# Two attention stages in another order, and the rotary tables moved behind the first feed-forward stage

## The reference

```python
def sublayer(x, shift, scale, gate, g_pre, g_post, fn, res_weight):
    h = rmsnorm(x, g_pre) * (1 + scale[:, None, :]) + shift[:, None, :]
    return x + res_weight * gate[:, None, :] * rmsnorm(fn(h), g_post)

# GLA, 4 heads, key width 128, value width 256, chunks of 64 tokens
q, k, v, log_a = chunks(q) * DK ** -0.5, chunks(k), chunks(v), chunks(log_a)
b = jnp.cumsum(log_a, axis=3)
q_dec = q * jnp.exp(b)
k_dec = k * jnp.exp(-b)
att = jnp.where(causal, jnp.einsum('bhnid,bhnjd->bhnij', q_dec, k_dec), 0.0)
o_intra = jnp.einsum('bhnij,bhnjv->bhniv', att, v)
upd = jnp.einsum('bhncd,bhncv->bhndv', k * jnp.exp(b_last - b), v)
# state scan over chunks: state = dec * state + upd
o = o_intra + jnp.einsum('bhncd,bhndv->bhncv', q_dec, states)
...
o = rmsnorm(o, g_out).astype(h.dtype).reshape(B, S, vd)
return (o * jax.nn.silu(r)) @ w_out

# MLA, 8 heads, 128 plain + 64 rotary columns, two blocks of 128 queries
c_q = rmsnorm(h @ w_dq, g_q)
q_nope, q_rope = jnp.split((c_q @ w_uq).reshape(B, S, MLA_HEADS, 192), [128], axis=-1)
q_rope = apply_rope(q_rope, cos, sin)
s = einsum(qn, k_nope) + einsum(qr, k_rope)   # scaled, masked
p = softmax(s)
o = einsum(p, v)
return o @ w_out
```

## Time and profile before

| what | value |
|---|---|
| time of the runs | 2954.34 us median of 3 (2954.05 to 2954.44) |
| profiled execution | 2955.43 us, its span 2953.7 us |
| PE busy | 2591.3 us, 88% of the span |
| DVE busy | 1575.9 us, 53% |
| ACT, POOL busy | 627.2 us, 681.8 us |
| mean granted TensorE clock | 0.963 |
| DMA | 928.84 MB, 314 GB/s over the span |

### The profile page before, as it was taken

One profiled execution on the slowest core, in us unless ns is written; L12 is line 12 of the kernel. 1 busy time (PEld: TensorE's weight loads), 2 busy tenths in 40 slices (PEclk: granted clock), 3 DMA queues, 4 the chain that ended last, 5 costly groups with the idle time before them and its releaser, 6 DMA issues.

```text
span 2953.7 us, 25930 instructions
## 1 busy us (share of the span) xinstructions
PE 2591.3 (88%) x9487; PEld 1600.5 (54%) x9487; DVE 1575.9 (53%) x3431; ACT 627.2 (21%) x1822; POOL 681.8 (23%) x687
## 2 busy tenths in 40 slices
PE   6999979998999789999889877898978999777776
PEld 4874548855884558847555422563634646322222
DVE  3562234633451435642378895546597466984444
ACT  1000201001000110000023333343333343332222
POOL 1110000100010001100024454323354243444332
PEclk8999989999999879999999999999999999999999
DMA  9994516955793517964179999999999999999997
GB/s 336 321 362 158 196 57 231 354 209 192 261 358 135 174 57 274 327 234 148 59 310 420 421 421 420 419 401 421 420 421 400 420 418 421 421 400 422 421 421 317
DMA packets 248998, 928.84 MB, mean 314 GB/s; under 512 B 19709, under 2 KB 120341, under 8 KB 167974
## 3 DMA queue, kind: packets, MB, share of 16 engines
q0 software_dynamic: 100768, 669.09, 55.9%
q1 hardware_dynamic: 148102, 258.08, 24.5%
HBM read 926.07 MB, written 1.05 MB: 314 GB/s over the span
## 4 chain that ended last, share of the span: by engine, by line
PE 62%; DMA 21%; DVE 10%; ACT 3%; issue 2%; SPq 1%; POOL 1%; DVEq 0%; POOLq 0%
DMA ring<-in_peer_uv_dram,lamt 20%; PE psW L871 19%; PE psF L824 13%; PE psF L1145 11%; PE psW L805 4%; DVE ring L2208 4%; PE psW L1215 3%; PE psW L774 2%; PE psW L794 2%; DMA mring<-in_tail_w_dram 1%; POOL ring L618 1%; PE psW L1227 1%; ACT small L1510 1%; PE psM L700 1%; PE psW L1166 1%
## 5 line engine op out<-in xcount | busy, mean ns | idle before, releaser
L1145 PE MATMUL psF<-ring,p_diag 128*128 128x512 f32 x2048 | 961.9, 615 | 232.8 <-ACT p_diag L1514 232.6
L2208 DVE SCALAR_TENSOR_TENSOR ring<-ring,h 128x1024 f32<-128x1024 f32 x512 | 621.3, 1224 | 442.0 <-DMA ring<-in_peer_uv_dram,lamt 438.5
L618 POOL DMA_INDIRECT ring<-in_peer_uv_dram,lamt x512 | 579.5, 1132 | 1045.0 <-PE psF L1145 812.8
L1145 PEld LDWEIGHTS psF<-ring,p_diag 128*128 128x128 f32 x2048 | 381.1, 195 | 763.6 <-issue 391.5
L871 PE MATMUL psW<-hT,ring 128*128 128x256 f32 x2560 | 556.6, 379 | 0.0
L871 PEld LDWEIGHTS psW<-hT,ring 128*128 128x128 f32 x2560 | 486.1, 190 | 74.9 <-issue 10.0
L824 PE MATMUL psF<-ring,arena 128*128 128x512 f32 x768 | 335.0, 597 | 15.1 <-DVE arena L2137 11.9
L824 PEld LDWEIGHTS psF<-ring,arena 128*128 128x128 f32 x768 | 146.6, 191 | 200.8 <-issue 183.2
L1507 ACT ACTIVATE small<-small 128x2 f32<-128x2 f32 x256 | 52.0, 203 | 733.5 <-DVE ring L2208 733.4
L1514 ACT ACTIVATE p_diag<-ident,small 128x128 f32<-128x128 f32 x512 | 177.6, 394 | 8.4
L1400 ACT ACTIVATE arena<-psW 128x256 f32<-128x256 f32 x88 | 33.8, 384 | 603.5 <-PE psW L871 539.8
(11 more groups left out here) (297 smaller groups left out, 2116.2 us busy)
## 6 DMA issues: line engine op xcount, KB each, us to landing
ring<-in_ffn_w_gu_dram SPq DMA_DIRECT2D x88, 1024.0 KB, 8.1
mring<-in_tail_w_dram SPq DMA_DIRECT2D x56, 1024.0 KB, 9.1
mring<-in_mod_t_dram POOLq DMA_DIRECT2D x43, 1024.0 KB, 7.2
ring<-in_ffn_w_down_dram SPq DMA_DIRECT2D x20, 2048.0 KB, 9.5
mring<-in_ada_w_dram POOLq DMA_DIRECT2D x22, 1024.0 KB, 7.6
M<-in_mod_t_dram POOLq DMA_DIRECT2D x21, 1024.0 KB, 7.2
mring<-in_cond_w_dram POOLq DMA_DIRECT2D x17, 1024.0 KB, 8.7
ring<-in_gla_w_in_dram SPq DMA_DIRECT2D x6, 2048.0 KB, 8.9
```

Source lines behind the costliest of these rows:

```text
L618: pool.indirect_dma_start(out=pair(n % PAIRS), out_offset=None, in_=rows, in_offset=bass.IndirectOffsetOnAxis(ap=s_idx[:, c:c + 1], axis=0 ...
L1145: ins = pe.matmul(psF[:, b, f * HALF:(f + 1) * HALF], p_diag[:, n % PAIRS, :], row_v(n % PAIRS)[:, f * HALF:(f + 1) * HALF], start=(i == 0 ...
L2208: dve.scalar_tensor_tensor(row_u(c), row_u(c), 1.0, h[:, b, :], ALU.mult, ALU.mult, accum_out=p_dots[:, c:c + 1]).then_inc(dot_done, 1)
```

## The change

Four edits.

1. DVE's table code and ACT's two functions for it become `tables()`, and are called once the first stage's `ffn` has returned, that is behind its last `half_step` on DVE and its last Silu on ACT, and ahead of the stage's finish.
2. In gla the two k units are not copied. DVE multiplies each straight out of its PSUM bank, `g_eu` first, then `g_en`. `state_ready` 2 follows the second `g_eu` product, and a new count 3 the last `g_en` product; PE waits for 3 ahead of the scores. ACT takes the roots of half 0 when its two output units are stored, and those of half 1 later; DVE scales and gates each half by itself (`scaled_heads`); PE turns half 0, projects it, turns half 1, projects it (`project_block`).
3. In mla the rotary columns come before the plain ones, in the loads and on PE, and DVE's two rotations stand between the stores of the plain columns.
4. The attention loop of mla makes two scores ahead; in a step PE does turn(s), score(s + 2), value(s), and DVE masks s + 2 between the copy of the turned probabilities and the store of the value.

```diff
@@ stage_loads, mla
-            yield [(slot(i + 1, 3, D)[:, k, :].rearrange("p (h c) -> p h c", c=NOPE), w[:, k, :, 0:NOPE])
-                   for k in range(3)], st.u + 11
-            yield [(slot(i + 2, 3, 512)[:, k, :].rearrange("p (h c) -> p h c", c=ROPE), w[:, k, :, NOPE:])
+            yield [(slot(i + 1, 3, 512)[:, k, :].rearrange("p (h c) -> p h c", c=ROPE), w[:, k, :, NOPE:])
+                   for k in range(3)], st.u + 9
+            yield [(slot(i + 2, 3, D)[:, k, :].rearrange("p (h c) -> p h c", c=NOPE), w[:, k, :, 0:NOPE])
                    for k in range(3)], st.u + 13
@@ PE
+        def project_block(i, lhs, b):
+
+            for k in range(KD):
+                if b == 0 and k % 4 == 0:
+                    arrived(i + k // 4)
+                w = slot(i + k // 4, 4, D)
+                for f in range(2):
+                    ins = pe.matmul(psF[:, b, f * HALF:(f + 1) * HALF], lhs[:, k, b * P:(b + 1) * P],
+                                    w[:, k % 4, f * HALF:(f + 1) * HALF], start=(k == 0), stop=(k == KD - 1))
+                if b == 1 and k % 4 == 3:
+                    ins.then_inc(w_used, 1)
+                if b == 0 and k == KD - 1:
+                    ins.then_inc(first_ready, 1)
@@ PE gla, ahead of the scores
+            pe.wait_ge(state_ready, 3)
@@ PE gla, end
-            u = transposes(u)
-            have(u - 1)
-            project(st, i + 7, hT, KD)
+            for b in range(TB):
+                u = turn_block(u, b)
+                have(u - 1)
+                project_block(i + 7, hT, b)
@@ PE mla
-            u = by_weights(u, slot(i + 1, 3, D), m_cT, 3, 8)
+            u = by_tokens(u, slot(i + 1, 3, 512), m_cT, 3, 512)
             arrived(i + 2)
-            u = by_tokens(u, slot(i + 2, 3, 512), m_cT, 3, 512)
+            u = by_weights(u, slot(i + 2, 3, D), m_cT, 3, 8)
@@ PE mla, loop
-            score(u, *steps[0])
-            u += 1
+            for s in range(2):
+                score(u, *steps[s])
+                u += 1
             for s, (b, g) in enumerate(steps):
-                if s + 1 < len(steps):
-                    score(u, *steps[s + 1])
+                turn(u, s, b)
+                turned = u
+                u += 1
+                if s + 2 < len(steps):
+                    score(u, *steps[s + 2])
                     u += 1
-                turn(u, s, b)
-                value(u + 1, s, b, g)
-                u += 2
+                value(u, s, b, g, turned)
+                u += 1
@@ ACT gla
-            have(st.u + 34)
-            roots_of(lambda j: h[:, j // 4, (j % 4) * GDV:(j % 4 + 1) * GDV], stats, 8, GDV,
-                     lambda j: g_junk[:, j, :])
+            for b in range(TB):
+                have(st.u + 32 + 2 * b)
+                roots_of(lambda j: h[:, b, j * GDV:(j + 1) * GDV], stats[:, 4 * b:4 * b + 4], 4, GDV,
+                         lambda j: g_junk[:, 4 * b + j, :])
@@ ACT, and likewise DVE with its table code
         for st in stages:
             table[st.kind](st)
+            if st.n == 0:
+                tables()
@@ DVE
+        def scaled_heads(b):
+
+            from_act()
+            root = stats[:, 4 * b:4 * b + 4]
+            link(dve.reciprocal(root, root))
+            for hd in range(GH):
+                o = h[:, b, hd * GDV:(hd + 1) * GDV]
+                ins = dve.scalar_tensor_tensor(o, o, root[:, hd:hd + 1], gout[:], ALU.mult, ALU.mult)
+            link(ins)
+            dve.tensor_tensor(h[:, b, :], h[:, b, :], g_r[:, b, :], ALU.mult).then_inc(h_ready, 1)
@@ DVE gla
-            dve.tensor_tensor(g_en, g_k, g_en, ALU.mult)
-            dve.tensor_tensor(g_eu, g_k, g_eu, ALU.mult).then_inc(state_ready, 1)
+            for g in range(2):
+                k_raw = full(u)[:].rearrange("p (a b) -> p a b", a=2)
+                heads = slice(2 * g, 2 * g + 2)
+                ins = dve.tensor_tensor(g_eu[:, heads], k_raw, g_eu[:, heads], ALU.mult)
+                if g == 1:
+                    ins.then_inc(state_ready, 1)
+                dve.tensor_tensor(g_en[:, heads], k_raw, g_en[:, heads], ALU.mult).then_inc(unit_stored, 1)
+                u += 1
+            dve.wait_ge(unit_stored, u)
+            dve.sem_inc(state_ready, 1)
@@ DVE gla, end
+                if b:
+                    scaled_heads(0)
+            scaled_heads(1)
             u = store_turned(u)
@@ DVE mla
-            u = masked(u, 0)
+            for s in range(2):
+                u = masked(u, s)
             for s in range(8):
                 b, g = divmod(s, 4)
-                if s + 1 < 8:
-                    u = masked(u, s + 1)
...
                 u = store(u, dst, src)
+                if s + 2 < 8:
+                    u = masked(u, s + 2)
```

More of the change, by code:

```diff
@@ L1046, in turn, with value @@
                 ins.then_inc(unit_full, 1)
-            def value(u, s, b, g):
-                have(u - 1)
+            def value(u, s, b, g, turned):
+                have(turned)
                 ps = open_unit(u)
@@ L2063, in mla @@
                 u = store(u, m_cT[:, :, b * P:(b + 1) * P], psW[u % 3][:, 0:QL].rearrange("p (a b) -> p a b", a=3))
-            for g in range(4):
-                u = store(u, m_qnT[:, 2 * g:2 * g + 2, :], psW[u % 3][:].rearrange("p (a b) -> p a b", a=2))
             for b in range(TB):
```

88 lines of the change are left out of this document (41 added, 47 removed).

## The result

The changed kernel takes 2906.53 us (median of 4 runs, 2904.5 to 2908.1), against 2954.2 us for the kernel before on the same chip. The ratio is 0.984 with a 95% interval of 0.983 to 0.986. That is 48 us less.

What follows compares the result with a forecast made beforehand. PE's matmuls were taken to bound the kernel, with winnable gaps where PE waits for DVE; 9.5 (first stage), 9.3 (GLA) and 16.5 (MLA) sum to 35.3 us, giving 2919.0 against the median 2954.34, range 2908 to 2931.

Steps and rivals of the forecast that it cites:

- all three places: PE's gaps in the first feed-forward stage, GLA's chain from last key product to output projection, and MLA.
- Part 1: First feed-forward stage: with the tables moved out, PE begins weight slot 1 earlier, less a cold restart; 9.5 us.
- Part 2: GLA: key products straight from PSUM bring the transposes 3.8 us earlier, and a kept clock gives 1.3 more.
- Part 3: GLA's norm and projection by token half: projection starts 6.1 us earlier, 1.9 given back inside it; net 4.2.
- GLA together: Gated attention in all: 3.8 from key products, 1.3 from clock, 4.2 from norm and projection by half; 9.3 us.
- Part 4: MLA before its first score: rotary matmuls first hide both rotations under the other matmuls; scores 5.0 us earlier.
- Part 5: MLA loop, scores two steps ahead: 8.1 us less waiting and 3 from the clock, taken as 11; projection behind, 0.5.
- The clock gives all: Rival: first stage, GLA and MLA gain their upper clock values, 50.1 us in all, 2904; chance 12 in 100.
- The clock gives nothing: Rival: MLA's loop stays at half speed and GLA's chain too; 27.7 us gained, 2926.6; chance 18 in 100.
- loads hold the first stage: Rival: PE loses at later weight slots what it gained at slot 1; 25.8 us left, 2928.5; chance 10 in 100.
- the band of 0.55 to 0.85: Sign: the MLA loop's granted clock leaving this band would show the forecast wrong.

Runs made afterwards that it cites:

- e8_small: The changed kernel with the ten small loads issued behind the loads of weight slots 1 to 3, no longer ahead of them: 2903.75 us.
- e2_rope: The kernel before with only the latent attention's rotary product, loads and rotations put first, its attention loop as before: 2944.03 us.
- e4_mla: The kernel before with both latent attention changes, rotary part first and scores two steps ahead, and none of the others: 2929.02 us.
- e7_idle: The kernel before, order kept, with unread 128x128 matmuls added ahead of turns and values in the latent attention's loop: 2937.34 us.
- e10_both: The changed kernel with unread matmuls in PE's waits ahead of the tail and the small loads moved behind weight slots 1 to 3: 2895.37 us.
- e3_ahead: The kernel before with only the latent attention loop's new order, scores two steps ahead: 2935.67 us.

## Why the forecast was off, point by point

- **What bounds the kernel.** Right: all three places were the right ones, and what was won at the front arrived at the end (the rest behind mla moved by 1.8 us of 1852).
- **Part 1, 9.5 us.** Right: 9.2 in the changed kernel and 9.7 alone. Slot 1's second part landed at 56.6 instead of the 56.5 of the estimate, PE waited for it for 5.3 us, and the cold restart cost 2.5 (30.33 against 27.8) where 2.4 was taken. That the load binds is shown by e8_small.
- **Part 2, 3.8 + 1.3.** Right within its bounds. The wait shrank by 3.8 exactly; the following 10.9 us became 8.7, so the clock gave 2.2 there, near the upper bound, but 1.4 of it was taken back in the output products.
- **Part 3, 4.2.** Right: 4.5 alone. The projection starts 6.4 us earlier, and 2.0 are given back between its halves (1.04 of transposes and 0.94 of waiting).
- **GLA together, 9.3.** Measured 8.5.
- **Part 4, 5.0.** The mechanism was right and exact: from the end of the last product to the first score it was 7.1 us and is 2.0. But the stage before the loop gained 7.8, and 8.0 in e2_rope; the other 2.8 are a low stretch of the clock that the kernel before and e4_mla have ahead of this place, and the changed kernel and e2_rope have not. Against e7_idle, which has the code of before here and took 43.40 us, the gain is 5.0. The forecast had no term for it, and that it fell this way is luck.
- **Part 5, 11 in the loop.** This is the step that failed: the loop gave 18.9, because the term of 3 us for the clock was too small. It had two terms, 8.1 for less idle time and 3 for the clock. Read as the forecast defined them, PE's waits fell by 5.0 us and its busy time by 13.9. e7_idle gives at most 7.7 for the order and at least 11.2 for the clock; the two readings differ because at full clock PE comes to a wait sooner and stands there longer (the first turn waits 1.56 us behind scores at half clock and 1.71 behind scores at full clock). The idle term was thus too large as waiting time: I took 1.24 us for each wait ahead of a turn, as in the last step of before. In the middle steps it is up to 2.12, because DVE takes the mask (L2121) and the maximum (L2126) of the score two steps ahead before the scaling (L2137), which the working left out:

```profile
1002.67 0.69 DVE L2121 SCALAR_TENSOR_TENSOR arena<-psW,arena 128x512 f32<-128x512 f32 x1 [1.30 <-PE psW L1052]
1003.39 0.69 DVE L2126 TENSOR_REDUCE small<-arena 128x2 f32<-128x512 f32 x1
...
1004.52 0.62 DVE L2137 TENSOR_SCALAR arena<-arena,small 128x256 f32<-128x256 f32 x2
```

  The clock term was mis-sized by nearly a factor of four, by the smaller of the two readings. I had a sum of the loop at full clock, 37, and one at half, 51.7, and took 46, near their middle, because of the one row in which a busy stretch had stayed at 0.52. The loop measured 37.9: the full clock in all but its last two steps. The projection gave 0.6 as taken (0.5).
- **The rivals.** "The clock gives all" came nearest with 2904, at 12 in 100. In the MLA loop it is what happened. It was held too unlikely with the argument that "the gaps of 1.2 us remain in each step"; they remained, larger even, and the clock fell for them only in the last two steps. In gla it was not so: 8.5 us there against the 10.5 of this rival. "The clock gives nothing" was held likelier, at 18, and is the further off: 2926.6. That loads hold the first stage came to the 5.3 us at slot 1 that the sum had in it, and PE waited for no later slot. DVE waited for modulation halves twice, 5.9 us together, and PE stood still for none of it.
- **The signs.** Right were the wait of 5.3 us ended by slot 1, the 0.8 us ahead of the GLA transposes, the cut projection with 0.94 us of idle time, the waits for the rotations that are gone, and the tables, which stand on DVE from 226 to 232 us beside the first projection. The turns wait 1.24 to 2.12 us, more than the 1.2 to 1.8 named. And one sign of being wrong came: the loop's granted clock, 0.92, left the band of 0.55 to 0.85.
- **The range.** The loop's miss alone would not have left it: with 18.9 for 11 the sum gives 2911.1, and even the loop's own bound of 20 gives 2910. What took the time below 2908 is that more came on top of it, the 2.8 us of clock ahead of the loop and the 2.9 us in stretches that had no term. Taken together, the loop's 7.9, these 2.8 and 2.9, and some 1 us less than summed in the other parts, make the 12.7 us by which the traces' 48.0 exceed 35.3. A range with the fully fast clock in it, which was priced at 2904 and left out, would have held the result.

## What to carry to other kernels

Where PE works in short pieces with waits of 1 to 2 us between, cost the stretch at both clocks, and don't settle in the middle without a reason: the loop here ran at 0.65 in one order and at 0.92 in another, with the waits of PE only a quarter shorter. Look at idle time per step against the work per step, and at whether two waits stand in one step; the value wait, hidden by the score that was put ahead of it, was only 0.65 us each. (That it is the second wait which matters is a guess; no run here takes it out by itself.) Where a wait can't be taken away, unread matmuls into a free bank held the clock here (1.00 in the loop of e10_both) and cost next to nothing where they ended before what PE waited for; but each wait that they bring themselves (here for the bank) must be one that is over by then. And before a cold stretch is counted as a loss, ask whether the engine that it waits for would be any earlier.

## What the runs showed of the hardware beyond the expected

- 19.2 us of added matmuls made a stretch of 56.8 us with its projection 13.8 us shorter (e7_idle); the granted clock of the loop rose from 0.65 to 0.93.
- The clock came back inside a loop without being helped: e3_ahead does its first two scores at half clock (0.63 for a pair of rows, PE busy without a gap for 3.8 us), waits 1.56, and has full clock in the next step (0.39).
- Neither the level at which PE enters a loop nor a single wait decided what the loop ran at: e2_rope entered at full clock and lost it within one step; the changed kernel went through a wait of 2.12 us in the loop at full clock, while 1.14 us of wait in gla, behind a piece in which DVE and PE took turns, was followed by output products at half clock:

```profile
380.00:382.00 2.00, 1.60 (x8) 1.05 (x6) 2.00 (x6) 0.00 (x0) 0.00 (x0) 1.00 0.42 127
382.00:384.00 2.00, 1.26 (x3) 0.61 (x4) 0.69 (x2) 0.00 (x0) 0.00 (x0) 0.62 0.01 2
384.00:386.00 2.00, 2.00 (x4) 0.69 (x4) 0.00 (x0) 0.00 (x0) 0.00 (x0) 0.50 0.00 0
```

  These are stretches of the changed kernel, with the columns of the earlier trace rows. What exactly makes the clock fall in one of such places and not in the other stays open; no run here tells it.
- Identical instructions with nearly identical waits took 38.3 us in one kernel and 41.1 in another (pre-loop of e2_rope and e4_mla), and 46.25 and 43.40 in the kernel before and e7_idle, by where the clock was low. The clock was low inside busy stretches too: 96 rows of products that PE did without a gap took 41.47 us in the changed kernel and 43.54 in e8_small.
